# A two-layer hybrid encoder trunk: x also passed transposed, loads by k-tile, the row scale folded into the rotary rows

## The reference

```
h    = x * rsqrt(mean(x*x) + 1e-6) * norm_g          # per token
proj = h @ w_in                                       # 1024 x 7936
a_q, a_k, a_v, a_gate, b_u, b_v, b_gate, c_q, c_f, c_i, c_gate, merge = split(proj)
out_a = sliding_window_attention(rope(a_q), rope(a_k), a_v) * silu(a_gate)
out_b = spatial_gating(gelu(b_u), gelu(b_v)) * silu(b_gate)
out_c = rmsnorm(hgrn2(c_q, sigmoid(c_f), c_i)) * silu(c_gate)
x    = x + (sum over branches of sigmoid(merge + b_merge) * (out @ w_branch)) @ w_out
```

## Time and profile before

| | |
|---|---|
| median of three runs | 1004.77 us (1004.13 to 1005.16) |
| profiled execution, its own time | 1005.19 us |
| its span, first to last instruction | 1003.4 us |
| TensorE busy | 993.5 us, 99% |
| VectorE, ScalarE, GpSimd busy | 624.4, 496.8, 290.7 us |
| mean granted TensorE clock | 0.997 |

### The profile page before, as it was taken

One profiled execution on the slowest core, in us unless ns is written; L12 is line 12 of the kernel. 1 busy time (PEld: TensorE's weight loads), 2 busy tenths in 40 slices (PEclk: granted clock), 3 DMA queues, 4 the chain that ended last, 5 costly groups with the idle time before them and its releaser, 6 DMA issues.

```text
span 1003.4 us, 15882 instructions
## 1 busy us (share of the span) xinstructions
PE 993.5 (99%) x6662; PEld 839.5 (84%) x6662; DVE 624.4 (62%) x864; ACT 496.8 (50%) x833; POOL 290.7 (29%) x148
## 2 busy tenths in 40 slices
PE   8999999999999999999999999999999999999997
PEld 7888998888888888888888989988888888888886
DVE  6889976897535353536638798488954535353652
ACT  6976576665523232223366766566554232323333
POOL 2322215324313232324112121162243232223330
PEclk9999999999999999999999999999999999999999
DMA  6432232222133232324233222321222323232602
GB/s 225 123 111 63 75 106 84 84 75 89 32 102 102 87 121 79 115 70 140 85 116 102 68 85 87 105 85 55 80 98 81 109 77 110 67 120 82 195 1 84
DMA packets 91639, 94.73 MB, mean 94 GB/s; under 512 B 2272, under 2 KB 89520, under 8 KB 91568
## 3 DMA queue, kind: packets, MB, share of 16 engines
q1 hardware_dynamic: 91440, 93.68, 29.8%
q10 hardware_dynamic: 128, 0.04, 0.0%
HBM read 91.62 MB, written 2.10 MB: 93 GB/s over the span
## 4 chain that ended last, share of the span: by engine, by line
PE 98%; issue 0%; DVE 0%; ACT 0%; POOL 0%; DVEq 0%; ACTq 0%; POOLq 0%
PE pj L537 29%; PE pj L539 28%; PE pj L538 28%; PE mx L537 2%; PE mx L538 2%; PE mx L539 2%; PE mx L637 1%; PE mx L737 1%; PE mx L614 1%; PE mx L683 1%; PE mx L711 1%; PE mx L622 1%; PE mx L714 1%; PE mx L701 1%; PE mx L496 0%
## 5 line engine op out<-in xcount | busy, mean ns | idle before, releaser
L1191 POOL TENSOR_TENSOR w_lo<-w_raw,w_hi 128x1024 fp32r<-128x1024 f32 (+1 forms) x89 | 197.9, 2224 | 546.7 <-ACT w_hi L855 546.7
L537 PE MATMUL pj<-h_hi,w_hi 128*128 128x512 f32 x832 | 328.2, 394 | 0.0
L539 PE MATMUL pj<-h_hi,w_lo 128*128 128x512 f32 x832 | 324.2, 390 | 0.0
L538 PE MATMUL pj<-h_lo,w_hi 128*128 128x512 f32 x832 | 324.0, 389 | 0.0
L855 ACT ACTIVATE w_hi<-w_raw 128x1024 fp32r<-128x1024 f32 (+1 forms) x179 | 159.0, 937 | 163.6 <-PE pj L539 163.6
L1302 DVE TENSOR_TENSOR w_lo<-w_raw,w_hi 128x1024 fp32r<-128x1024 f32 (+1 forms) x90 | 173.1, 1923 | 81.1 <-ACT w_hi L855 80.8
L537 PEld LDWEIGHTS pj<-h_hi,w_hi 128*128 128x128 f32 x832 | 156.2, 188 | 33.1 <-issue 1.4
L539 PEld LDWEIGHTS pj<-h_hi,w_lo 128*128 128x128 f32 x832 | 156.2, 188 | 33.0
L538 PEld LDWEIGHTS pj<-h_lo,w_hi 128*128 128x128 f32 x832 | 156.3, 188 | 31.2
L1412 DVE TENSOR_TENSOR merge_gate<-pj,rstd 128x512 f32<-128x512 f32 x48 | 33.2, 691 | 164.5 <-PE pj L539 164.5
L973 ACT ACTIVATE merge_gate<-merge_gate,small 128x512 f32<-128x512 f32 x48 | 34.3, 715 | 92.7 <-DVE merge_gate L1412 92.7
(11 more groups left out here) (270 smaller groups left out, 1416.1 us busy)
## 6 DMA issues: line engine op xcount, KB each, us to landing
w_raw<-in_w_in SPq DMA_DIRECT2D x61, 1024.0 KB, 5.5
w_raw<-in_w_branch SPq DMA_DIRECT2D x24, 512.0 KB, 3.4
w_raw<-in_w_out SPq DMA_DIRECT2D x6, 1024.0 KB, 5.2
x_tokens<-in_x SPq DMA_DIRECT2D x4, 512.0 KB, 6.6
w_raw_last<-in_w_out SPq DMA_DIRECT2D x2, 1024.0 KB, 7.4
sp_wT<-in_sp_w SPq DMA_DIRECT2D x2, 512.0 KB, 3.7
out<-out_low SPq DMA_DIRECT2D x4, 256.0 KB, 2.0
out<-out_high SPq DMA_DIRECT2D x4, 256.0 KB, 2.3
```

The lines of the kernel that those rows point to most:

```text
L537: pe.matmul(bank, wh, ah, start=first, stop=False)
L538: pe.matmul(bank, wh, al, start=False, stop=False)
L539: return pe.matmul(bank, wl, ah, start=False, stop=final)
L1191: return pool.tensor_tensor(out=dst, in0=full, in1=hi.bitcast(f32), op=ALU.subtract)
```

## The change

Two more arrays are passed in: `xT`, x with its axes exchanged, and `vecs`, the norm, bias and gate vectors with channels first. (hgrn_lb, b_merge, hgrn_norm_g and norm_g themselves are no longer passed.) The transposes and copies of the opening are gone. SyncE loads `xT` by k-tile, 256 KB each, in turn with parts of units 0 and 1, then the positions, unit 2, and after that the four loads of `x_tokens`. The first quarter of the token statistics moves to VectorE's job 0, the other three to its job 3, with `rstd_diagonal` and `trig`; ScalarE's root moves from job 0 to job 3, its sines stay at job 2, its copy of the row moves to job 4; TensorE's rstd matmuls move from after job 2 to after job 3. In the rope, `cos` and `sin` are multiplied by `rstd` once, at the first rope of a layer, and the multiplication at the end of each of the five ropes is dropped. The scores wait for the ropes one by one.

```diff
@@ SyncE: loads
             sp.dma_start(CST[:, :], consts[:, :]).then_inc(cst_in, 16)
-            load_x(0)
+            load_xT(0)
             sp.dma_start(buf[:, 0:2, :], src[:, 0:2, :]).then_inc(first_in[0], 16)
-            load_x(1)
+            load_xT(1)
+            load_xT(2)
             sp.dma_start(buf[:, 2:4, :], src[:, 2:4, :]).then_inc(first_in[1], 16)
-            load_x(2)
+            load_xT(3)
             sp.dma_start(buf[:, 4:8, :], src[:, 4:8, :]).then_inc(raw_in[0], 16)
-            load_x(3)
-            load_weights(sp, 1)
+            load_xT(4)
+            load_xT(5)
+            buf, src = unit_load(1)
+            sp.dma_start(buf[:, 0:4, :], src[:, 0:4, :]).then_inc(first_in[2], 16)
+            load_xT(6)
+            load_xT(7)
+            sp.dma_start(buf[:, 4:8, :], src[:, 4:8, :]).then_inc(raw_in[1], 16)
             sp.dma_start(POSI[:, :], positions[0].partition_broadcast(P)).then_inc(pos_in, 16)
             load_weights(sp, 2)
+            for j in range(KT // 2):
+                load_x(j)
@@ TensorE: opening, rstd, scores
+            def small_warm(count):
+                for _ in range(count):
+                    pe.matmul(M[0][0:16, P:P + 16], ONE[:, 0:16], ONE[:, 0:16], start=True, stop=True)
+
             pe.wait_ge(fill_done, 1)
-            warm(4)
...
-            warm(5)
-            transpose_x(0)
-            transpose_x(1)
...
+            warm(10)
+            small_warm(22)
...
-                    if n == 2 and layer == 0:
-                        pe.wait_ge(xT_evac, KT)
-                        pe.wait_ge(fill_done, 1)
+                    if n == 3 and layer == 0:
                         pe.wait_ge(p_diag, 1)
                         for tb in range(TB):
                             last = pe.matmul(M[4][:, tb * P:(tb + 1) * P], ONE[:, :], DG[:, tb, :],
...
+                    pe.wait_ge(rope_done, upto(rope_done, j + 2))
                     if j == 0:
-                        pe.wait_ge(rope_done, upto(rope_done, 5))
@@ ScalarE: lists
                 if layer == 0:
-                    phase[0].append((first_rstd,))
-                    phase[2].append((rstd_row,))
-                    phase[2].append((bounds_exp,))
                     phase[2].append((first_sines,))
+                    phase[3].append((first_rstd,))
+                    phase[4].append((bounds_exp,))
+                    phase[4].insert(0, (rstd_row,))
@@ GpSimd: the first half of unit 1 goes to VectorE
-            split_lo(1)
-
@@ VectorE: statistics, lists, rope
+            def statistics():
+                for j in range(1, KT // 2):
+                    last = x_stats(j)
...
                 if layer == 0:
-                    phase[0].append((rstd_diagonal,))
+                    phase[0].append((x_stats, 0))
                     phase[0].append((angle_rest,))
-                    phase[2].append((trig,))
+                    phase[3].append((statistics,))
+                    phase[3].append((rstd_diagonal,))
+                    phase[3].append((trig,))
...
+                        dve.tensor_tensor(out=COSR[:, :], in0=COS[:, :], in1=RS[:, :], op=ALU.mult)
+                        chained(dve.tensor_tensor(out=SINR[:, :], in0=SIN[:, :], in1=RS[:, :], op=ALU.mult))
                     dst = QP[:, r - 1, :] if r >= 1 else KP[:, :]
-                    dve.tensor_tensor(out=R1[:, :], in0=QR[:, r % 3, :], in1=COS[:, :], op=ALU.mult)
-                    chained(dve.tensor_tensor(out=R2[:, :], in0=QS[:, r % 3, :], in1=SIN[:, :], op=ALU.mult))
-                    chained(dve.tensor_tensor(out=R1[:, :], in0=R1[:, :], in1=R2[:, :], op=ALU.add))
-                    dve.tensor_tensor(out=dst, in0=R1[:, :], in1=RS[:, :], op=ALU.mult).then_inc(rope_done, 1)
+                    dve.tensor_tensor(out=R1[:, :], in0=QR[:, r % 3, :], in1=COSR[:, :], op=ALU.mult)
+                    chained(dve.tensor_tensor(out=R2[:, :], in0=QS[:, r % 3, :], in1=SINR[:, :], op=ALU.mult))
+                    dve.tensor_tensor(out=dst, in0=R1[:, :], in1=R2[:, :], op=ALU.add).then_inc(rope_done, 1)
```

More of the change, by code:

```diff
@@ L103, in constants, with build @@
     return c
-def build(nc, x, positions, w_in, b_merge, w_branch, w_out, norm_g, final_g, attn_sinks, sp_w, sp_b,
-          sp_ln_g, sp_ln_b, hgrn_lb, hgrn_norm_g, consts, out):
+def build(nc, x, xT, vecs, positions, w_in, w_branch, w_out, final_g, attn_sinks, sp_w, sp_b,
+          sp_ln_g, sp_ln_b, consts, out):
     f32, f32r, i32 = mybir.dt.float32, mybir.dt.float32r, mybir.dt.int32
@@ L295, in build @@
         x_in = [sem(f"x_in{j}") for j in range(KT // 2)]
-        norm_in, vec_in, cst_in, pos_in = sem("norm_in"), sem("vec_in"), sem("cst_in"), sem("pos_in")
-        first_in = [sem(f"first_in{q}") for q in range(2)]
+        vec_in, lb_in, cst_in, pos_in = sem("vec_in"), sem("lb_in"), sem("cst_in"), sem("pos_in")
+        first_in = [sem(f"first_in{q}") for q in range(3)]
         quarter_hi, quarter_lo = sem("quarter_hi"), sem("quarter_lo")
-        fill_done, xT_done, xT_evac = sem("fill_done"), sem("xT_done"), sem("xT_evac")
+        fill_done = sem("fill_done")
+        xT_in = [sem(f"xT_in{k}") for k in range(KT)]
         pro_step = sem("pro_step")
         p_half, p_turns = sem("p_half"), sem("p_turns")
-        normT_done, p_norm, p_vec = sem("normT_done"), sem("p_norm"), sem("p_vec")
         p_bounds = sem("p_bounds")
         p_ms, p_root, p_rstd, p_diag = sem("p_ms"), sem("p_root"), sem("p_rstd"), sem("p_diag")
-        vecT_done, p_diff, p_exp, p_trig, p_sin = sem("vecT_done"), sem("p_diff"), sem("p_exp"), sem("p_trig"), sem("p_sin")
+        p_diff, p_exp, p_trig, p_sin = sem("p_diff"), sem("p_exp"), sem("p_trig"), sem("p_sin")
         fg_in = sem("fg_in")
@@ L482, in _ @@
         def _(pe):
[L484 to L492, removed]
             def warm(count):
@@ L868, in first_h @@
             def first_h(k):
[L869 to L874, removed]
+                act.wait_ge(xT_in[k], 16)
+                scaled_hi(k, 0).then_inc(xg_hi, 1)
             act.wait_ge(fill_done, 1)
             act.activation(RO[:, 0:1], EP, ACT.Copy)
-            act.wait_ge(p_norm, 1)
+            act.wait_ge(vec_in, 16)
             def quarter(q):
@@ L898, in _ @@
             first_h(5)
+            act.wait_ge(first_in[2], 16)
+            split_half(1, 0)
             first_h(6)
             first_h(7)
[L901 to L907, removed]
+            weights_in(act, 1)
+            split_half(1, 1)
             def rsqrt(dst, src, scale):
@@ L1320, in x_stats @@
                 return last
-            dve.wait_ge(normT_done, 1)
-            dve.tensor_copy(VL[:, :, 0:8], M[1][:, 0:16].rearrange("p (l c) -> p l c", l=2)).then_inc(p_norm, 1)
-            dve.wait_ge(p_norm, 1)
             dve.wait_ge(cst_in, 16)
[L1326 to L1329, removed]
+            dve.wait_ge(vec_in, 16)
             first_low(0)
@@ L1332, in _ @@
             first_low(1)
-            x_stats(0)
             first_low(2)
@@ L1336, in _ @@
             first_low(3)
-            x_stats(1)
+            first_low(4)
             split_half(0, 1)
-            first_low(4)
             first_low(5)
-            x_stats(2)
             first_low(6)
+            dve.wait_ge(w_hi, 3)
+            dve.tensor_tensor(out=lo_part(1, 0), in0=raw_part(1, 0), in1=hi_part(1, 0).bitcast(f32),
+                              op=ALU.subtract).then_inc(w_lo, 2)
             first_low(7)
-            split_lo(1)
-            pchain(x_stats(3))
-            for tb in range(TB):
-                last = dve.bn_aggr(MV[:, tb, :], XS[:, tb, :, :])
-            pchain(last)
-            pchain(dve.tensor_tensor(out=MS, in0=MV[:, :, 0], in1=MV[:, :, 0], op=ALU.mult))
-            dve.tensor_tensor(out=MS, in0=MS, in1=MV[:, :, 1], op=ALU.add).then_inc(p_ms, 1)
-            dve.wait_ge(p_vec, 1)
+            split_half(1, 1)
+            dve.wait_ge(lb_in, 16)
             L0, L1, mx = LBT[:, 24:28], LBT[:, 28:32], LBT[:, 0:4]
@@ L1364, in trig @@
                 dve.wait_ge(p_trig, 1)
+            def statistics():
+                for j in range(1, KT // 2):
+                    last = x_stats(j)
+                pchain(last)
+                for tb in range(TB):
+                    last = dve.bn_aggr(MV[:, tb, :], XS[:, tb, :, :])
+                pchain(last)
+                pchain(dve.tensor_tensor(out=MS, in0=MV[:, :, 0], in1=MV[:, :, 0], op=ALU.mult))
+                dve.tensor_tensor(out=MS, in0=MS, in1=MV[:, :, 1], op=ALU.add).then_inc(p_ms, 1)
             def rstd_diagonal():
@@ L1853 @@
     arrays["in_consts"] = constants()
+    cols = {n: arrays.pop(f"in_{n}").reshape(DEPTH, -1, P) for n in ("norm_g", "b_merge", "hgrn_norm_g", "hgrn_lb")}
+    per_layer = _np.concatenate([cols["norm_g"], cols["b_merge"], cols["hgrn_norm_g"]], axis=1)
+    rows = _np.concatenate([per_layer.reshape(-1, P), cols["hgrn_lb"].reshape(-1, P)])
+    arrays["in_vecs"] = _np.ascontiguousarray(rows.T)
```

(1 more changed line is left out.)

42 lines of the change are left out of this document (11 added, 31 removed).

## The result

The changed kernel takes 1008.6 us (median of 7 runs, 1008.45 to 1009.57), the kernel before beside it 1004.8 us (1004.13 to 1005.4); the ratio is 1.0042 with an interval of 1.0031 to 1.0052. The forecast was 1007.7 us, slower. The profiled execution took 1008.45 us by its own time with a span of 1006.7 us, 3.3 us more than the span of before.

The account below looks back on a forecast made before the run. TensorE, busy 993.5 of 1003.4 us, bounds the kernel; a late rstd chain to 37.25 plus 2.1 us half clock gives 39.35 against 36.47, 2.9 later: 1007.7 us, 8-in-10 range 1002.6 to 1009.6.

Parts of the forecast that it names:

- Opening: TensorE's start without the x transposes: first matmul at 7 to 9, unit 0 done at 19.5 against 24.64, some 5 us gained.
- Step 1: First load of x by tokens, now behind x^T, units 0 to 2 and positions: lands at 21.0, bounds 20.2 and 22.4.
- Steps 2 and 3: VectorE's first-quarter statistics end at 22.45, then its angle work, stretched beside GpSimd's split, gives p_half at 28.0.
- the meeting: VectorE's angle work overlapping GpSimd's weight split of unit 2: claimed to lengthen the angle work by 2.2 us.
- Step 4: ScalarE's queue after p_half: sines until 30.65, copy-out of job 2 until 33.7, then table load and root, done at 35.25.
- Step 5: VectorE's branch into the root: split of unit 2 and remaining statistics, ready at 34.5, slightly ahead of ScalarE's 34.95.
- the first rival: Same chain but shorter, through no meeting, earlier loads or little clock cost: no change, 1004.7 to 1005.6 us; chance 0.34.
- Step 6: Reciprocal and diagonal on VectorE, then rstd matmuls from 36.35 to 37.25, with TensorE standing about 5.9 us.
- the clock: TensorE at half clock for 4.2 us after its stop, losing 2.1 us; bounds nothing to 3.1.
- Sum: TensorE past four jobs and the rstd matmuls at 39.35 against 36.47, 2.9 us later, giving 1007.7 us.
- the yardstick: When TensorE gets past four jobs and the rstd matmuls, 36.47 before; both programs give it the same work afterwards.
- Downstream: After the rstd matmuls: no second TensorE stop, the split of unit 3 done 1 to 2 us before it is needed.

Follow-up runs that it names:

- experiments 4: Changed kernel with the rope as before, multiplied by rstd at the end of each rope: 1009.24 us, ratio 1.0040 to the kernel before.
- experiment 5: Changed kernel, same loads, with VectorE's statistics ahead of the angles and ScalarE's root ahead of the sines: 1007.36 us, ratio 1.0021 to the kernel before.
- experiment 2: Changed kernel with eight more warm matmuls ahead of TensorE's first data: 1009.19 us, ratio 1.0042 to the kernel before.
- experiment 3: Changed kernel with GpSimd's split of unit 2 held until VectorE's angles are done: 1006.4 us, ratio 1.0015 to the kernel before.
- experiment 1: Changed kernel with 27 extra matmuls of ones filling TensorE's wait ahead of the rstd matmuls: 1006.48 us, ratio 1.0012 to the kernel before.
- experiments 3 and 6: The second: changed kernel with positions and token loads issued earlier, angles, statistics, sines and root moved to earlier jobs: 1002.79 us, ratio 0.9982 to the kernel before.

## Why the prediction was right, and where it wasn't

- *Opening.* Unit 0 was forecast to end at 19.5 and ended at 19.38; the first matmul, at 6.90, came just ahead of the 7 to 9. That unit 0's end fits so well is in part luck: with the same opening it came at 22.11 and 21.48 in the traces of experiments 4 and 5, outside the 18.3 to 20.5. That it isn't part of the sum was shown by experiment 2.
- *Step 1.* The first token load landed at 21.80, 0.8 later than the 21.0 I took and within its bounds; 21.4, the plain count of bytes, would have been nearer. The estimate that larger rows might bring it forward found no support.
- *Steps 2 and 3.* Angles by GpSimd were done at 22.57 (22.6), statistics of the first quarter at 23.23 (22.45), the meeting stretched the angle work to 5.3 us (5.55), `p_half` at 28.54 (28.0). Experiment 3 prices the meeting at 2.1 us, for the 2.2 taken.
- *Step 4.* ScalarE stood 4.34 us ahead of the sine's table load (about 3 forecast), and the root was done at 35.80 (35.25). The rule on a drain with the table load (the Trainium skill, ScalarE: Activation LUTs, "What ACT_TABLE_LOAD costs") finds no more support after than before: sine and root start 0.01 us behind the two loads of 1.28 us, and the root's load starts 0.02 us behind the copy-out ahead of it.
- *Step 5.* The mean squares came at 34.66 (34.5), 0.8 us before ScalarE was through its table load (0.45 forecast). "Speeding up one branch alone gives back at most half a microsecond" was tried by no run. But the use that I made of it in the theory of experiment 3 was wrong: I took the meeting for a delay of one branch, and taking it away gave back its whole 2.1 us. My own working began the VectorE branch at the same 28.0 that held the 2.2 us: the angle work is no branch of its own but the common stem of both, since the statistics queue behind it on VectorE. The price that the first rival put on the meeting (1005.5 for 1007.7, 2.2 less) was the right one.
- *Step 6 and the clock.* The rstd matmuls started at 36.78 (36.35), after a stop of 6.4 us (5.9), and half clock lasted 4.3 us (4.2), which cost 2.1 us (2.1) by experiment 1.
- *Sum.* Forecast 2.9 us later at the yardstick, measured 3.27 at the scores. The late load of step 1 is the reason: it put the statistics 0.8 us back, the angle work made up 0.25 of that, and steps 4 and 6 took about what was forecast, so that the rstd matmuls came 0.4 late. The medians differ by 3.8, as the profiled execution of before lay 0.4 above its median and that of after 0.15 below it. The forecast took the 0.42 of before off the time after, too, and after has no such offset; that is the rest of the 0.9 us between 1007.7 and 1008.6.
- *Downstream.* No second stop followed, as forecast. The split of unit 3 was done at 48.70 and TensorE came to job 6 at 51.20, 2.5 us of slack (1 to 2 forecast); experiment 5, with the angles 5.6 us later, used it up.
- *The rope fold* was costed at nothing; the kernel without it was not measurably faster or slower, and TensorE waits for a rope in neither. VectorE's half of the split of unit 1, taken over from GpSimd, has no place in the sum and was not tried alone; VectorE stood idle for 2.10 us ahead of the first statistics, waiting for their load, so it is not on the chain.

The rivals: the shorter chain needed the meeting gone, which experiment 3 had to force; ScalarE alone setting the wait needed p_half by 23.3, and in the changed kernel the first quarter of x had only just been counted then.

## What to carry over

When TensorE is 99% busy, a faster opening is worth only what the next thing that TensorE waits for comes earlier: follow that chain through the queues of the other engines before counting the gain. A step put off because its user comes later takes with it everything that it is then queued behind; two chains that share one queue have a common stem, and a delay there counts for both. And price a stop of TensorE with the slower clock behind it: here 6.4 us of standing cost another 2.1.

## What the runs showed of the hardware

- The granted clock also fell after work had resumed. In experiment 5 TensorE stood from 44.75 to 48.15 at 1.00, worked at 1.00 in the slice from 48, and got 0.50 from about 49.4 to 52.8. Stops of 6.4, 6.2, 4.2 and 3.4 us were followed by half clock, as the 1.9 us ahead of the first data were the earlier trace rows, and the 1.9 us ahead of the fifth k-tile in experiments 4 and 5; those of 1.1, 1.2 and 1.3 us were not.
- When a VectorE operation with two inputs and a GpSimd split overlapped, the one that began later was the longer one: 2.78 us for 0.70 on VectorE, 3.25 for 2.41 on GpSimd. VectorE's batch statistics, with one input, kept their 0.33 us each beside the split (experiments 3 and 6).
- One and the same opening differs between executions: of the five traces that have it as the changed kernel does, three have unit 0 end at 19.26 to 19.38 and two at 21.48 and 22.11, the two in which the stop ahead of the fifth k-tile was 1.9 us.
